# Rotating before normalising, block-by-block first panels and moved roundings in a three-layer fp32 block

## The reference

```python
def rms_norm(x, g):
    xf = x.astype(jnp.float32)
    y = xf * lax.rsqrt(jnp.mean(xf * xf, axis=-1, keepdims=True) + EPS)
    return (y * g.astype(jnp.float32)).astype(x.dtype)

def diff_mixer(h, cos, sin, layer_depth, w_in, q_gain, k_gain, ...):
    q, k, v = jnp.split(h @ w_in, [DIFF_W, 2 * DIFF_W], axis=-1)
    q = apply_partial_rope(rms_norm(q.reshape(B, S, DIFF_HEADS, 2, dh), q_gain), cos, sin)
    k = apply_partial_rope(rms_norm(k.reshape(B, S, DIFF_HEADS, 2, dh), k_gain), cos, sin)
    ...
    p = masked_softmax(s, kpos[None, :] <= t[:, None])
    a = p[:, :, 0] - lam * p[:, :, 1]
    o = rms_norm(einsum(a, v), subln_g) * (1.0 - lam_init)

def second_block(x, c, ...):
    cond = jax.nn.silu(c)
    mod = cond @ w_ada[i] + b_ada[i]
    sh1, sc1, g1, sh2, sc2, g2 = jnp.split(mod, 6, axis=-1)
    h = rms_norm(x, ln_mix_g[i]) * (1.0 + sc1) + sh1
    x = x + g1 * mixer(h)
    ...                     # then the MLP, with sh2, sc2, g2 in the same way
```

## Time and profile before

| | us |
|---|---|
| median of 3 runs | 1504.69 (1503.11 to 1506.68) |
| profiled execution | 1499.84 |
| its span | 1498.2 |
| PE busy in it | 1438.1 |

### The profile page before, as it was taken

How to read it: one execution, slowest core, us unless ns; L and a number is a source line. 1 busy time by engine, 2 the same in 40 slices (tenths; PEclk the granted TensorE clock), 3 DMA queues, 4 the chain that set the end, 5 groups by cost and what they waited for, 6 DMA issues and landing times.

```text
span 1498.2 us, 26200 instructions
## 1 busy us (share of the span) xinstructions
PE 1438.1 (96%) x10989; PEld 1358.3 (91%) x10989; DVE 962.0 (64%) x1200; ACT 622.8 (42%) x783; POOL 75.8 (5%) x127
## 2 busy tenths in 40 slices
PE   7999999999999999999998899899999998999998
PEld 6999999888999999998986578899999876899998
DVE  5679877644677777666516855888875476555543
ACT  5444454343443343344612644343344325344341
POOL 4031000000000000101000000100000000000000
PEclk9999999999999999999967999999999989999999
DMA  8656444443478888855600024999965420256551
GB/s 232 191 189 196 144 147 146 141 141 127 164 262 273 278 266 272 267 190 161 211 28 0 1 73 154 305 301 305 312 207 169 155 85 1 84 170 188 179 194 57
DMA packets 172628, 260.92 MB, mean 174 GB/s; under 512 B 5125, under 2 KB 147634, under 8 KB 172418
## 3 DMA queue, kind: packets, MB, share of 16 engines
q1 hardware_dynamic: 160890, 203.13, 41.7%
q0 software_dynamic: 10816, 53.63, 10.8%
q10 hardware_dynamic: 840, 2.98, 0.6%
HBM read 258.67 MB, written 1.05 MB: 173 GB/s over the span
## 4 chain that ended last, share of the span: by engine, by line
PE 82%; DVE 11%; ACT 3%; issue 2%; DMA 2%; POOL 0%; DVEq 0%; ACTq 0%; SPq 0%; POOLq 0%
PE ring L658 62%; PE acc L658 18%; DVE w_lo L1691 1%; ACT w_hi L1242 1%; DVE arena L1744 1%; DVE arena L1836 1%; PE acc L1078 1%; DVE norm L1706 1%; ACT arena L1242 1%; PE ring L917 1%; DVE h_lo L1738 1%; DMA raw<-in_diff_w_in_dram 1%; DMA raw<-in_w_mlp_in_dram 1%; DVE arena L2206 1%; DVE arena L2203 1%
## 5 line engine op out<-in xcount | busy, mean ns | idle before, releaser
L1691 DVE TENSOR_TENSOR w_lo<-raw,w_hi 128x2048 fp32r<-128x2048 f32 (+1 forms) x191 | 437.0, 2289 | 331.7 <-ACT w_hi L1242 331.4
L658 PE MATMUL ring<-h_hi,w_hi 128*128 128x256 f32 x2088 | 598.3, 287 | 13.3 <-DVE h_lo L1738 8.8
L658 PE MATMUL ring<-h_lo,w_hi 128*128 128x256 f32 x2088 | 592.4, 284 | 0.0
L658 PE MATMUL ring<-h_hi,w_lo 128*128 128x256 f32 x2088 | 592.2, 284 | 0.0
L1242 ACT ACTIVATE w_hi<-raw 128x2048 fp32r<-128x2048 f32 (+1 forms) x191 | 363.5, 1904 | 230.5 <-DMA raw<-in_w_mlp_out_dram 60.0
L658 PEld LDWEIGHTS ring<-h_hi,w_hi 128*128 128x128 f32 x2088 | 402.3, 193 | 21.4 <-issue 10.4
L658 PEld LDWEIGHTS ring<-h_lo,w_hi 128*128 128x128 f32 x2088 | 402.5, 193 | 0.4
L658 PEld LDWEIGHTS ring<-h_hi,w_lo 128*128 128x128 f32 x2088 | 402.3, 193 | 0.0
L658 PE MATMUL acc<-e_hi,w_hi 128*128 128x256 f32 x768 | 219.2, 285 | 3.0 <-DVE e_lo L2332 3.0
L658 PE MATMUL acc<-e_lo,w_hi 128*128 128x256 f32 x768 | 217.6, 283 | 0.0
L658 PE MATMUL acc<-e_hi,w_lo 128*128 128x256 f32 x768 | 217.6, 283 | 0.0
(11 more groups left out here) (262 smaller groups left out, 1349.9 us busy)
## 6 DMA issues: line engine op xcount, KB each, us to landing
arena<-in_w_ada_dram POOLq DMA_DIRECT2D x64, 768.0 KB, 6.0
raw<-in_w_mlp_in_dram SPq DMA_DIRECT2D x32, 1024.0 KB, 5.5
raw<-in_w_mlp_out_dram SPq DMA_DIRECT2D x32, 1024.0 KB, 5.1
raw<-in_w_in_dram SPq DMA_DIRECT2D x24, 1024.0 KB, 5.2
raw<-in_w_e_gate_dram SPq DMA_DIRECT2D x16, 1024.0 KB, 5.5
raw<-in_w_e_up_dram SPq DMA_DIRECT2D x16, 1024.0 KB, 6.8
raw<-in_w_e_down_dram SPq DMA_DIRECT2D x16, 1024.0 KB, 6.5
raw<-in_diff_w_in_dram SPq DMA_DIRECT2D x12, 1024.0 KB, 5.1
```

The lines of the kernel that those rows point to most:

```text
L658: return nc.tensor.matmul(dst, lhs, rhs, start=start, stop=stop, **kw)
L1691: tt(w_lo[q % SPL][:, 0:n], raw[q % RAW][:, 0:n], w_hi[q % SPL][:, 0:n].bitcast(F32), ALU.subtract)\
```

## The change

1. `split_norm`, `high_parts` and `h_ready` work by single blocks in all seven norms. PE runs the first panels by a new function, `linear_first`: the outer loop is over the blocks `k`, and inside it both halves of one panel (`a_gate`, `moe`, `mlp0`, `mlp1`) or of two panels (`x_q`, `n_q`, `d_q`). `keep_busy` has 10 copies instead of 11 ahead of `mlp0`, `mlp1` and `d_q`.
2. In the differential layer ACT multiplies the gain into queries and keys as it takes them from PSUM, and squares them from PSUM too. Each is rotated two panels after its own. The sums stand behind the first value panel; the spread factors are multiplied in behind the rotation. The 14 copies of `keep_busy` are gone.
3. The last rounding, `ahead(PN["d_o"])`, stands behind the heads on ACT and on DVE instead of ahead of them.
4. The first four modulation pieces of the second layer stand between the panels of `n_o` instead of behind the first chunk of `mlp0`.

```diff
+        PER_NORM = {"squared": 4, "summed": 1, "scaled": KB, "hi": KB, "ready": KB}
...
+            def linear_first(panels, f, ready):
+                for i in range(len(panels)):
+                    open_panel(panels[i])
+                    open_fill(f + i)
+                for k in range(KB):
+                    ready(k)
+                    for i, p in enumerate(panels):
+                        wh = w_hi[p % SPL][:].rearrange("p (k n) -> p k n", k=KB)
+                        wl = w_lo[p % SPL][:].rearrange("p (k n) -> p k n", k=KB)
+                        for b in range(2):
+                            o, c = bank(f + i)[:, b * T:(b + 1) * T], slice(b * P, (b + 1) * P)
+                            mm(o, wh[:, k, c], h_hi[:, k, :], k == 0 and b == 0, False, skip_group_check=True)
+                            mm(o, wh[:, k, c], h_lo[:, k, :], False, False, skip_group_check=True)
+                            last = mm(o, wl[:, k, c], h_hi[:, k, :], False, k == KB - 1, skip_group_check=True)
+                        if k == KB - 1:
+                            last.then_inc(S("panel_done"), 1)
...
-            def full(name, ready=None, norm=None):
-                for i in range(FL_N[name]):
+            def block_ready(sem):
+                def ready(k):
+                    pe.wait_ge(*sig(sem, k + 1))
+                return ready
+            def full(name, ready=None, norm=None, split=None, together=2):
+                if split is not None:
+                    linear_first([PN[name] + i for i in range(together)], FL[name], block_ready(split))
+                for i in range(together if split is not None else 0, FL_N[name]):
...
-            full("x_q", h_ready("x_ready"))
+            full("x_q", split="x_ready")
...
+            pe.wait_ge(*sig("ffn_scaled", KB))
...
-            ready = h_ready("ffn_ready")
-            linear(PN["moe"], moe_fill(0), KB, 2, lambda k: h_hi[:, k, :], lambda k: h_lo[:, k, :], ready)
+            linear_first([PN["moe"]], moe_fill(0), block_ready("ffn_ready"))
...
-                linear(PN[name], FL[name], KB, 2, hi, lo, h_ready(f"m{l}_ready"))
+                keep_busy(FL[name], 10)
+                linear_first([PN[name]], FL[name], block_ready(f"m{l}_ready"))
...
-            keep_busy(FL["d_q"], 11)
-            full("d_q", h_ready("d_ready"))
-            full("d_k")
-            def sq_d_ready(b):
-                pe.wait_ge(S("d_heads_squared"), b // 2 + 1)
-            row_sums("d_sums", 16, lambda b: blk(D_SQ, 16)[:, b], sq_d_ready)
+            keep_busy(FL["d_q"], 10)
+            linear_first([PN["d_q"], PN["d_q"] + 1], d_qk_fill(0), block_ready("d_ready"))
+            def d_panel(j):
+                linear(PN["d_q"] + j, d_qk_fill(j), KB, 2, lambda k: h_hi[:, k, :], lambda k: h_lo[:, k, :])
+            def rotate_d(j):
+                rotate("d_rope", j, blk(D_Q + 2 * j, 2), "d_evicted")
+            for j in range(2, 8):
+                d_panel(j)
+                rotate_d(j - 2)
+            rotate_d(6)
...
+            rotate_d(7)
+            row_sums("d_sums", 16, lambda b: blk(D_SQ, 16)[:, b], lambda b: drained_wait(pe, d_qk_fill(b // 2)))
...
-            for i in range(2):
-                linear_rows(PN["d_v"] + 2 + i, d_v_fill(2 + i))
-                for j in range(4 * i, 4 * i + 4):
-                    rotate("d_rope", j, blk(D_Q + 2 * j, 2), "d_normed")
+            for i in (2, 3):
+                linear_rows(PN["d_v"] + i, d_v_fill(i))
...
-            keep_busy(d_s_fill(0), 14)
-            pe.wait_ge(S("d_roped"), 8)
+            drained_wait(pe, FL["d_spread"] + 7)
...
-                for j in range(KB // 2):
-                    act.wait_ge(*sig(tag + "_scaled", j + 1))
+                for b in range(KB):
+                    act.wait_ge(*sig(tag + "_scaled", b + 1))
...
-                        func(hh[:, 2 * j:2 * j + 2, :], src[:, 2 * j:2 * j + 2], ACT.Copy).then_inc(S(tag + "_hi"), 1)
+                        func(hh[:, b, :], src[:, b], ACT.Copy).then_inc(S(tag + "_hi"), 1)
...
-                        for b in (2 * j, 2 * j + 1):
...
-                        last.then_inc(S(tag + "_hi"), 1)
+                        func(hh[:, b, :], src[:, b], ACT.Identity, bias=shift(b)).then_inc(S(tag + "_hi"), 1)
...
-            for name, at in (("d_q", D_Q), ("d_k", D_K)):
-                for i in range(4):
-                    take(name, i, blk(at, 8)[:, 2 * i:2 * i + 2])
-                    drained_wait(act, FL[name] + i)
-                    squares(blk(at, 8)[:, 2 * i:2 * i + 2], blk(at + D_SQ, 8)[:, 2 * i:2 * i + 2], "d_heads_squared")
+            act.wait_ge(S("d_gains"), 1)
+            for j in range(8):
+                p, f = PN["d_q"] + j, d_qk_fill(j)
+                ahead(p)
+                act.wait_ge(S("panel_done"), p + 1)
+                func(blk(D_Q + 2 * j, 2), bank(f)[:].rearrange("p (b t) -> p b t", b=2), ACT.Identity,
+                     scale=k_scaled[:, j // 4:j // 4 + 1]).then_inc(S("d_evicted"), 1)
+                func(blk(D_SQ + 2 * j, 2), bank(f)[:].rearrange("p (b t) -> p b t", b=2), ACT.Square)\
+                    .then_inc(S(f"drained{f % BANKS}"), 1)
+            func(note[:, 15:16], ones[:, 0:1], ACT.Sqrt)
...
-            ahead(PN["d_o"])
...
+            ahead(PN["d_o"])
...
-                def low(j):
-                    dve.wait_ge(*sig(tag + "_hi", j + 1))
-                    s = slice(2 * j, 2 * j + 2)
+                def low(b):
+                    dve.wait_ge(*sig(tag + "_hi", b + 1))
...
-                        last = tt(h_lo[:, s, :], blk(mid, 8)[:, s], h_hi[:, s, :].bitcast(F32), ALU.subtract)
+                        last = tt(h_lo[:, b, :], blk(mid, 8)[:, b], h_hi[:, b, :].bitcast(F32), ALU.subtract)
...
-                        for b in (2 * j, 2 * j + 1):
-                            last = stt(h_lo[:, b, :], blk(mid, 8)[:, b], shift(b), h_hi[:, b, :].bitcast(F32),
-                                       ALU.add, ALU.subtract)
+                        last = stt(h_lo[:, b, :], blk(mid, 8)[:, b], shift(b), h_hi[:, b, :].bitcast(F32), ALU.add, ALU.subtract)
...
-                for j in range(KB // 2):
-                    for b in (2 * j, 2 * j + 1):
-                        last = stt(blk(mid, 8)[:, b], x_t[:, b, :], gain(b), norm[:, row, :], ALU.mult, ALU.mult)
-                    last.then_inc(S(tag + "_scaled"), 1)
-                    if j:
-                        low(j - 1)
-                low(KB // 2 - 1)
+                for b in range(KB):
+                    stt(blk(mid, 8)[:, b], x_t[:, b, :], gain(b), norm[:, row, :], ALU.mult, ALU.mult)\
+                        .then_inc(S(tag + "_scaled"), 1)
+                    if b == 1:
+                        low(0)
+                    elif b > 2:
+                        low(b - 2)
+                low(KB - 2)
+                low(KB - 1)
...
+                    if behind is not None and i < 3:
+                        behind(i)
...
-            residual("n_o", scale=lambda b: mods[:, 0, 16 + b:17 + b])
+            def first_pieces(i):
+                for n in ((0,), (1, 2), (3,))[i]:
+                    ada(1, n)
+            residual("n_o", scale=lambda b: mods[:, 0, 16 + b:17 + b], behind=first_pieces)
...
-                    if l == 0 and c == 0:
-                        for n in range(ADA_FIRST):
-                            ada(1, n)
-                    elif l == 0 and ADA_FIRST + 2 * c - 2 < 2 * STEPS:
+                    if l == 0 and c and ADA_FIRST + 2 * c - 2 < 2 * STEPS:
...
+            chain.did(ts(k_scaled[:, 0:1], vcol("dq_gain"), HD ** -0.5, None, ALU.mult))
+            chain.did(nc.vector.tensor_copy(k_scaled[:, 1:2], vcol("dk_gain")))
+            chain.did(ts(k_scaled[:, 2:3], vcol("subln"), 1.0 - LAM_INIT, None, ALU.mult))
+            chain.settle()
...
-            chain.did(ts(k_scaled[:, 0:1], vcol("dq_gain"), HD ** -0.5, None, ALU.mult))
-            chain.did(nc.vector.tensor_copy(k_scaled[:, 1:2], vcol("dk_gain")))
-            chain.did(ts(k_scaled[:, 2:3], vcol("subln"), 1.0 - LAM_INIT, None, ALU.mult))
-            ahead(PN["d_v"] - 1)
-            ahead(PN["d_v"])
+            ahead(PN["d_q"] + 1)
+            ahead(PN["d_q"] + 2)
+            for j in range(8):
+                view = blk(D_Q + 2 * j, 2)
+                rope("d_rope", j, view, view, blk(D_TMP + 2 * (j % 2), 2), "d_roped")
+                if j < 7:
+                    ahead(PN["d_q"] + 3 + j)
...
-            ahead(PN["d_v"] + 1)
-            chain.settle()
+            dve.wait_ge(S("d_roped"), 8)
...
+                f = FL["d_spread"] + j
...
-                head_norm("d_spread", j, view, k_scaled[:, j // 4:j // 4 + 1], None)
-                nc.vector.tensor_copy(note[:, 8:9], view[:, 0, 0:1]).then_inc(S("d_normed"), 1)
-            for j in range(8):
-                if j % 4 == 0:
-                    ahead(PN["d_v"] + 2 + j // 4)
-                view = blk(D_Q + 2 * j, 2)
```

(7 more changed lines are left out.)

27 lines of the change are left out of this document (13 added, 14 removed).

## The result

| | before | after |
|---|---|---|
| median of 4 runs, us | 1505.68 (1503.11 to 1506.72) | 1483.21 (1481.55 to 1488.42) |
| profiled execution | 1499.84 | 1483.57 |
| its span | 1498.2 | 1481.9 |

The ratio of the times is 0.9859, with a 95% interval of 0.9831 to 0.9887: 17 to 25 us faster. The forecast was 1484.9 (1475 to 1495), 19.8 us faster. The two profiled executions are only 16.3 us apart; that of before was one of its shorter ones. Lines of the changed kernel's program are numbered some 30 higher (`mm` is L662, `w_lo` L1725, `h_lo` with a shift L1770).

A forecast was written before the change was run, and what follows sets the result against it. PE was busy 96% of the span, so time could come only from its idle gaps, low clock and keep_busy copies. The terms summed to +19.8 us, taking the median from 1504.69 to 1484.9, range 1475 to 1495.

The forecast's parts named there:

- First panels by blocks: At the norms' first panels, PE starts earlier: x_q +2.0, n_q +2.3, mlp0 and mlp1 +3.1 each, d_q +3.0 us.
- the middle between a clock that falls and one that stays: At n_q: +1.3 us if the clock stays low, +3.4 if the shorter gap keeps it up; +2.3 taken.
- ffn: Norm ahead of the router: the eighth scaling stands behind five small subtractions, 0.6 us lost (0 to 1.2).
- The split's price: On DVE in the norms: halving a 128x512 operation costs 0.19 us a piece; by the Trainium skill, 0.42 against 0.69 us.
- The two waits: In mlp0's first chunks, PE's waits of 2.57 and 4.11 us go, with 1.1 of low clock: +7.8 us.
- part of it comes back: -2.4: In mlp0, raw panels are late sooner, 318 GB/s asked against 315 seen: 2.4 us lost (0 to 5).
- rival B: mlp0 is held by its transfers and PE waits later for as much: 5.4 us less, 14.4 gained, 1490; chance 20%.
- The new wait: Ahead of the head sums' spread, PE idles 2.6 us for the reciprocal, queued on DVE behind a rounding and a rotation.
- a colder start of the spread: 1.0 (0 and 1.7): In the differential layer, the spread starts at a lower clock: 1.0 us lost, estimated from n_q, bounds 0 and 1.7.
- 1.4 us of tail: Behind the differential layer's last key panel, 1.4 us left over, mostly low clock around 1200, counted again after the change.
- -1.2: Behind the heads, the moved rounding stands ahead of root and reciprocal: 1.2 us lost (0.8 to 2.5).
- +0.7: At the heads' start, the rounding no longer stands ahead of the first maximum on DVE: 0.7 us gained (0 to 1).

The follow-up runs named there:

- p1_blocks: Kernel before with part 1 alone (norms and first panels by blocks, ten keep_busy copies instead of eleven): 1493.03 us, ratio 0.9914.
- e1_root: Changed kernel with DVE's rounding of panel d_o 0 put behind the reciprocal of the head sums: 1478.77 us, ratio to before 0.9824.
- e6_wide: On top of e1_root, all 128 rows of the spread table in the differential layer's spread matmuls instead of 32: 1472.68 us, ratio 0.9799.
- p2_diff: Kernel before with part 2 alone, the differential layer: 1505.23 us against 1501.21, ratio 1.0023.
- p4_pieces: Kernel before with part 4 alone, the first four modulation pieces moved into n_o: 1493.28 us, ratio 0.9922.
- e3_do_early: Changed kernel with part 3 undone, the last rounding ahead of the heads again on both engines: 1482.69 us, ratio 0.9863.

## Why the prediction was right, and where only by luck

The total was right: 1484.9 forecast, 1483.21 measured. The terms were not equally good, and two misses of 4.4 and 3.3 us lie on opposite sides: that the total came so near is luck. What is not luck are the first panels and the pieces, which bring most of the time in the way that was forecast.

- **First panels by blocks.** Right in mechanism and size: `x_q` 2.3 (2.0), `n_q` 1.8 (2.3), `mlp0` 2.5 (2.8 with `n_o`), `d_q` 3.6 and 3.2 (3.0), `mlp1` 2.5 (3.1). p1_blocks confirms them without the other parts. For `n_q` I took the middle between a clock that falls and one that stays. Both happen behind the same 2.30 us of idle PE: it fell in the profiled execution and stayed up in two others, and 1.4 us hang on it. At `ffn` the table's loss is 1.6 and not 0.6: the wait was sized well (0.62 became 1.27), the clock behind it was not counted. That part differs between executions: the stretch took 81.7 to 82.0 us in three traces with the program of before, and 82.4 to 85.2 in seven with the wait of 1.27.
- **The split's price.** The changed kernel's 24 subtractions of 128x256 (least, median and most ns in the row shown) took 0.417 us, against 0.685 for the twelve of 128x512 before: 0.15 us a pair. The Trainium skill, "VectorE: DVE Perf Modes", section on the TRN2 errata, gives 0.424 and 0.691 by its formula; the trace agrees. Its advice against small tiles did not decide here: with the split `x_q` gained 2.3 where 2.0 were forecast, since PE's blocks of 1.44 us leave DVE the room.

```profile
L1768 DVE TENSOR_TENSOR h_lo<-arena,h_hi x24: 412/417/426, 20.8 to 377.2; 128x256 fp32r<-128x256 f32 x24
```

- **`mlp0`.** The two waits were worth what they showed, 8.7 with the clock. The step that failed is "part of it comes back: -2.4", and with it rival B. I set 318 GB/s of demand against the 315 of one stretch and took the second for a limit. It was only what the kernel had asked for: the changed one moved 345 in the same ten microseconds. The kernel before had moved as much itself, a little later:

```profile
968.00:976.00 8.00, 8.00 (x70) 8.00 (x69) 4.83 (x4) 4.74 (x4) 0.53 (x1) 1.00 0.97 345
```

A rate seen under a kernel that waits bounds the limit from below.
- **The differential layer.** The new wait was right in place and size (2.46, forecast 2.6), read off the order of the lists alone. The step that failed is "a colder start of the spread: 1.0 (0 and 1.7)". The spread took 13.5 us where 8.66 + 1.0 were reckoned, and the value panel behind it ran 4 us at half clock. The bound came from `n_q`, where the work behind the gap holds 128 rows; the spread holds 32, and e1_root and e6_wide show that, without any wait, this is what lets the clock go; the wait makes it go sooner (13.5 us against 11.05). And 8.66 was the shortest of the three executions that have the spread as before. The earlier trace rows had the sign of it: the kernel before was at 0.50 around 1200 with no idle PE ahead of it. I took that for 1.4 us of tail, not for a property of the spread. So part 2 alone is no gain but some 0.2% slower (p2_diff), with its 6.2 us of copies paid out again.
- **Last rounding.** -1.2 stood in the traces as -1.1, once the 1.6 us of clock are taken out. +0.7 was met by the pair of profiled executions alone: the heads took 31.06 us in that of before, but 32.5 in p1_blocks and p4_pieces, with the same program and the same wait there. On the changed layer the rounding is worth 3.4 (e3_do_early), as PE's wait with it is 5.2 us and not 2.5.
- **What else the table shows.** Of the -3.1 at the start 2.2 stand in p4_pieces too, whose program is that of before there; so does all of the +3.4 ahead of the sparse attention, and 1.5 to 1.7 us more in the heads and behind them. With p4_pieces as the measure wherever it has the program of before, the stretches sum to 18.4 us for the change instead of 16.3, at the near end of the timed 17 to 25. What the rest of the timed difference is, the traces don't say; the kernel before has executions from 1497.3 to 1508.8 us, and one of the lower ones was profiled.
